# Scan, attention and gathering in one block, and a feed-forward's last turn by token halves

## What is computed

```python
# second block
y_sc  = sc_b * causal_dwconv(sc_c * sc_h, w_sconv)                  # 256 wide
o     = gated_delta_rule_chunked(l2norm(gq), l2norm(gk), gv, g, beta)   # 4 heads of 128: the scan
y_gdn = rmsnorm(o, w_gdn_norm) * silu(gz)                           # 512 wide: the gating
y_sb  = stick_breaking_attention(sq, sk, sv)                        # 4 heads of 64
x = x + concatenate([y_sc, y_gdn, y_sb]) @ w_mix_out                # 1024 x 1024
u = causal_dwconv(rmsnorm(x, w_norm_ffn) @ w_ffn_up, w_ffn_conv)    # 3 taps; first block: no convolution
gate, val = split(u)                                                # 2816 each
x = x + (silu(gate) * val) @ w_ffn_down
out = rmsnorm(x, w_norm_final)
# stick breaking: A[t,s] = sigmoid(z_ts) * prod_{s<j<t} (1 - sigmoid(z_tj)), z = q.k/sqrt(64), s < t
```

## Time and profile before

| | |
|---|---|
| median of 3 runs | 2931.18 us (2931.16 to 2939.09) |
| profiled execution | 2928.09 us, span of the core 2926.4 us |
| TensorE busy | 2715.1 us, 93% |
| VectorE, ACT, POOL busy | 1306.2 (45%), 658.8 (23%), 1150.9 us (39%) |
| mean granted TensorE clock | 0.974 of full speed |

### The profile page before, as it was taken

How to read it: one execution, slowest core, us unless ns; L and a number is a source line. 1 busy time by engine, 2 the same in 40 slices (tenths; PEclk the granted TensorE clock), 3 DMA queues, 4 the chain that set the end, 5 groups by cost and what they waited for, 6 DMA issues and landing times. The chain is left out here.

```text
span 2926.4 us, 35051 instructions
## 1 busy us (share of the span) xinstructions
PE 2715.1 (93%) x12987; PEld 2175.6 (74%) x12987; DVE 1306.2 (45%) x1819; ACT 658.8 (23%) x1173; POOL 1150.9 (39%) x901
## 2 busy tenths in 40 slices
PE   4999887999999999969999888879899999999996
PEld 2888446888888888857888677854588888888885
DVE  4022542323343333371351356667234555666556
ACT  2110661300010000051232233235222211111113
POOL 2443026234444444433454323200523554555551
PEclk9999998999999999989999899989999999999998
DMA  3110103111111111121111000000311111111111
GB/s 103 44 51 27 40 15 130 29 44 47 47 50 50 47 50 47 57 73 47 51 47 44 1 1 1 1 1 1 130 30 37 49 44 49 50 50 47 50 54 65
DMA packets 91204, 131.53 MB, mean 45 GB/s; under 512 B 9461, under 2 KB 57824, under 8 KB 91112
## 3 DMA queue, kind: packets, MB, share of 16 engines
q1 hardware_dynamic: 88808, 121.88, 13.9%
q10 hardware_dynamic: 2304, 8.39, 0.7%
HBM read 121.82 MB, written 8.42 MB: 45 GB/s over the span
## 5 line engine op out<-in xcount | busy, mean ns | idle before, releaser
L123 POOL TENSOR_TENSOR w_hi<-w_raw,zero 128x512 fp32r<-128x512 f32 x352 | 417.6, 1186 | 1198.4 <-PE bank L980 473.5
L125 POOL TENSOR_TENSOR w_lo<-w_raw,w_hi 128x512 fp32r<-128x512 f32 x352 | 511.8, 1454 | 27.6
L978 PE MATMUL bank<-xt_hi,w_hi 128*128 128x512 f32 x1312 | 510.6, 389 | 1.6 <-DVE x_sb L1156 0.8
L979 PE MATMUL bank<-xt_lo,w_hi 128*128 128x512 f32 x1312 | 510.4, 389 | 0.0
L980 PE MATMUL bank<-xt_hi,w_lo 128*128 128x512 f32 x1312 | 510.4, 389 | 0.0
L1254 DVE TENSOR_TENSOR x_sb<-bank,x_sb 128x512 f32<-128x512 f32 x320 | 221.3, 691 | 213.9 <-PE bank L1014 213.9
L978 PEld LDWEIGHTS bank<-xt_hi,w_hi 128*128 128x128 f32 x1312 | 246.3, 188 | 53.5 <-DVE x_sb L1156 1.3
L980 PEld LDWEIGHTS bank<-xt_hi,w_lo 128*128 128x128 f32 x1312 | 246.3, 188 | 51.2
L979 PEld LDWEIGHTS bank<-xt_lo,w_hi 128*128 128x128 f32 x1312 | 246.3, 188 | 51.0
L177 PE MATMUL bank<-xt_hi,w_hi 128*128 128x512 f32 x512 | 199.4, 389 | 0.0
L177 PE MATMUL bank<-xt_lo,w_hi 128*128 128x512 f32 x512 | 199.2, 389 | 0.0
(11 more groups left out here) (412 smaller groups left out, 4513.2 us busy)
## 6 DMA issues: line engine op xcount, KB each, us to landing
w_raw<-in_w_gate_up_dram SPq DMA_DIRECT2D x88, 256.0 KB, 3.1
w_raw<-in_w_ffn_up_dram SPq DMA_DIRECT2D x88, 256.0 KB, 3.1
w_raw<-in_w_mix_in_dram SPq DMA_DIRECT2D x48, 256.0 KB, 2.7
w_raw<-in_w_down_dram SPq DMA_DIRECT2D x44, 256.0 KB, 2.6
w_raw<-in_w_ffn_down_dram SPq DMA_DIRECT2D x44, 256.0 KB, 2.6
w_raw<-in_w_in_dram SPq DMA_DIRECT2D x40, 256.0 KB, 2.7
x_sb<-in_x_dram SPq DMA_DIRECT2D x8, 512.0 KB, 7.3
gate_rows<-gate_sums SPq DMA_DIRECT2D x8, 512.0 KB, 4.9
```

Of the source, the lines that this page charges most:

```text
L123: pool.tensor_tensor(m.w_hi[:, u, :], m.w_raw[:, u, :], zeros, ALU.add).then_inc(m.hi_done, 1)
L125: pool.tensor_tensor(m.w_lo[:, u, :], m.w_raw[:, u, :], m.w_hi[:, u, :].bitcast(F32), ALU.subtract).then_inc(m.split, 1)
L978: pe.matmul(m.psum[b][:, :], u_hi[:, col], m.xt_hi[:, k, tok], start=k == 0, stop=False)
L979: pe.matmul(m.psum[b][:, :], u_hi[:, col], m.xt_lo[:, k, tok], start=False, stop=False)
```

## The change

1. `scan_stage`, `stick_stage` and `gather_stage` become one block, `read_stage`. The attention's buffers get addresses of their own. The last chunk's update of the state is left out. In the scan ACT squares each head's output with an accumulated sum just behind its copy, for the 1/rms. POOL scales and gates `gz`, eight tiles each, makes the convolution's `xt_lo` and splits the next stage's first four slices, which SP loads. ACT rounds the convolution's rows. Finished attention outputs go from the bank into `xt_hi` (ACT) and `xt_lo` (VectorE) at once. The transposes of `gz` stand in the last two steps (first four groups) and behind them (last four), in the banks of the scores.
2. In both `mlp_stage`s the loop has a pass less. The last up product takes token half 0 through all eight slices, then half 1. Slices 4 to 7 go to `end_hi`, `end_lo`, so that all eight stay in SBUF; the last hidden rows go to `last_hi`, `last_lo`. ACT and VectorE make half 0 of the last hidden rows beside half 1 of the up product, and half 1 beside the down product before the last, VectorE with a step after each bank that it reads. POOL's split for the next stage waits until the last rescale.
3. In `proj2_stage` the chunk made of two column pieces is loaded with one DMA per slice.

The diff, cut (in `read_stage`, `L` is the number of steps):

```diff
+    end_hi, end_lo = m.at("end_hi" + tag, [P, 4, HALF], 152, F32R), m.at("end_lo" + tag, [P, 4, HALF], 160, F32R)
+    last_hi, last_lo = m.at("last_hi" + tag, [P, 2, S], 168, F32R), m.at("last_lo" + tag, [P, 2, S], 8, F32R)
+    spare = [m.at(f"scaled_out{i}" + tag, [P, 4, D], (16, 152)[i]) for i in range(2)]
...
-            with sp.Fori(0, FI - 1) as i:
+            with sp.Fori(0, FI - 2) as i:
                 up_slices(loop + 12 * i, i + 1)
                 down_slices(loop + GU + 12 * i, i)
+            up_slices(last, FI - 1)
+            down_slices(last + GU, FI - 2)
...
-            down_slices(loop + 12 * (FI - 1), FI - 1)
+            down_slices(last + 12, FI - 1)
...
-            split_slices(m, pool, loop, 12 * FI - 8)
+            split_slices(m, pool, loop, 12 * (FI - 2))
+            for k in range(GU):
+                u, n = k % RING, last + k
+                if k < RING:
+                    split_slice(m, pool, n, n // RING, u, False)
+                else:
+                    pool.wait_ge(m.loaded[u], 16 * (n // RING) + 16)
+                    pool.tensor_tensor(end_hi[:, u, :], m.w_raw[:, u, :], zeros, ALU.add).then_inc(m.hi_done, 1)
+                    pool.wait_ge(m.hi_done, n + 1)
+                    pool.tensor_tensor(end_lo[:, u, :], m.w_raw[:, u, :], end_hi[:, u, :].bitcast(F32),
+                                       ALU.subtract).then_inc(m.split, 1)
+            for u in range(DN):
+                n = last + GU + u
+                pool.wait_ge(m.used, last + u + 1)
+                split_slice(m, pool, n, n // RING, u, True)
+            split_slices(m, pool, last + 12, DN)
...
+                pool.wait_ge(scl, 2 * NT)
...
                 up(loop + 12 * i, wait_bank)
                 down(loop + GU + 12 * i, i)
-            pe.wait_ge(m.split, loop + 12 * (FI - 1) + 4)
+            for h in range(2):
+                for k in range(KD):
+                    pe.wait_ge(m.split, last + k + 1)
+                    for b in range(4 * h, 4 * h + 4):
+                        if k == 0:
+                            pe.wait_ge(ev_d if b % 2 else ev_a, 4 * (FI - 2) + b // 2 + 1)
+                            pe.wait_ge(dn_ev, 16 * (FI - 2) + b + 1)
+                        if k < RING:
+                            up_bank(last, k, m.w_hi[:, k, :], m.w_lo[:, k, :], b)
+                        else:
+                            up_bank(last, k, end_hi[:, k % RING, :], end_lo[:, k % RING, :], b)
+            down(last + GU, FI - 2)
+            pe.wait_ge(m.split, last + 12 + DN)
...
+            def finish_half(h):
+
+                i, tok = FI - 1, slice(h * HALF, (h + 1) * HALF)
+                if conv:
+                    act.wait_ge(ev_a, 4 * i + 2 * h + 2)
+                    act.wait_ge(ev_d, 4 * i + 2 * h + 2)
+                    for c in range(4):
+                        act.activation(mix[:, c, tok], raw[:, c, PAD + h * HALF:PAD + (h + 1) * HALF], ACT.Identity,
+                                       scale=weights_of(i, c, 2)).then_inc(tap, 1)
+                    for c in range(2):
+                        act.wait_ge(acted, 4 * i + 4 * h + c + 1)
+                        act.activation(mix[:, c, tok], mix[:, c, tok], ACT.Silu).then_inc(sig, 1)
+                for j in range(2):
+                    act.wait_ge(hid_a, 4 * i + 2 * h + j + 1)
+                    act.activation(last_hi[:, j, tok], mix[:, j, tok], ACT.Copy).then_inc(sig2, 1)
...
+                        if last_step is not None and NT * nh + t < STEPS:
+                            last_step(1, NT * nh + t)
...
+            TAPS = 8 if conv else 0
+            STEPS = TAPS + 4
+
+            def last_step(h, n):
...
+                i, tok = FI - 1, slice(h * HALF, (h + 1) * HALF)
+                pad = slice(PAD + h * HALF, PAD + (h + 1) * HALF)
+                j = n % 2
+                if n < TAPS:
+                    c, back = n // 2, 1 + j
+                    if back == 1:
+                        dve.wait_ge(tap, 4 * i + 4 * h + c + 1)
+                    else:
+                        dve.wait_ge(mid, 4 * i + 4 * h + c + 1)
+                    dve.scalar_tensor_tensor(
+                        mix[:, c, tok], raw[:, c, PAD - back + h * HALF:PAD - back + (h + 1) * HALF],
+                        weights_of(i, c, 2 - back), mix[:, c, tok], ALU.mult, ALU.add).then_inc(mid if back == 1 else acted, 1)
+                elif n < TAPS + 2:
+                    if conv:
+                        dve.wait_ge(acted, 4 * i + 4 * h + 4)
+                        dve.wait_ge(sig, 2 * i + 2 * h + 2)
+                    else:
+                        dve.wait_ge(ev_a, 4 * i + 2 * h + 2)
+                        dve.wait_ge(ev_d, 4 * i + 2 * h + 2)
+                    a_, u_ = (mix[:, j, tok], mix[:, 2 + j, tok]) if conv else (raw[:, j, pad], raw[:, 2 + j, pad])
+                    dve.tensor_tensor(mix[:, j, tok], a_, u_, ALU.mult).then_inc(hid_a, 1)
+                else:
+                    dve.wait_ge(hid_a, 4 * i + 2 * h + 2)
+                    dve.wait_ge(sig2, 4 * i + 2 * h + j + 1)
+                    dve.tensor_tensor(last_lo[:, j, tok], mix[:, j, tok], last_hi[:, j, tok].bitcast(F32),
+                                      ALU.subtract).then_inc(hid, 1)
...
+            with dve.Fori(0, FI - 2) as i:
                 read_up(loop + 12 * i, i + 1)
                 read_down(loop + GU + 12 * i, i)
                 finish(i + 1)
+            read_up(last, FI - 1, (0, 1))
+            for n in range(STEPS):
+                last_step(0, n)
+            read_up(last, FI - 1, (2, 3))
+            read_down(last + GU, FI - 2, last_step)
...
+                    apart = pieces[c][1][0] - col
+                    before = apart - 256
+                    load_slices(m, sp, base, 8 * c, 8, lambda j, u: (
+                        m.w_raw[:, u, :].rearrange("p (s n) -> p s n", s=2),
+                        w[bass.ds((j * RING + u) * P, P), col - before:col - before + 2 * apart]
+                        .rearrange("p (s n) -> p s n", s=2)[:, :, before:apart]))
...
-            split_slices(m, pool, base, 32, RING)
-            for k in range(KD):
-
-                pool.wait_ge(two[k % RING], 16 * (k // RING + 1))
-                if k % RING == RING - 1:
-                    split_slices(m, pool, base + 32 + k - RING + 1, RING)
-            split_slices(m, pool, base + 40, 16)
+            split_slices(m, pool, base, 8 * NC, RING)
...
+def read_stage(m, q_, k_, v_, t_at, gz, sc, sqk, sv, first):
...
+    zc, sp, acc, A = (m.at(n, [P, 4, HALF], 120 + 8 * i) for i, n in enumerate(("z_capped", "softplus", "later", "weights")))
...
+            pool.wait_ge(rs_done, 2)
+            for c in range(NT):
+                g4 = gz[:, c, :].rearrange("p (h n) -> p h n", h=HG)
+                pool.tensor_tensor(g4, g4, rs[:, c, :].unsqueeze(2).to_broadcast([P, HG, P]), ALU.mult).then_inc(scaled, 1)
+            for c in range(NT):
+                pool.wait_ge(scaled, c + 1)
+                pool.tensor_tensor(gz[:, c, :], gz[:, c, :], o[:, c, :, :].rearrange("p h n -> p (h n)"),
+                                   ALU.mult).then_inc(gated, 1)
+            pool.wait_ge(gated, NT)
+            for k in range(2):
+                pool.wait_ge(sc_hi, k + 1)
+                pool.tensor_tensor(m.xt_lo[:, k, :], sc[:, k, :], m.xt_hi[:, k, :].bitcast(F32), ALU.subtract)
+            split_first(m, pool, m.slices)
...
+                if c < NT - 1:
+                    for h in range(HG):
+                        pe.matmul(m.psum[h][:, 0:P], kd[:, h, c, :], vn[:, h, :], start=True, stop=True).then_inc(pe_s, 1)
...
+                if p == 2:
+                    pe.wait_ge(act_s, 4 * NT)
...
+            def turn_gates(i):
+
+                h, k = i // 4, i % 4
+                if i < 6:
+                    pe.wait_ge(weighed, 2 * (L - 3 + i // 2) + i % 2 + 1)
+                else:
+                    pe.wait_ge(g_lo, i - 5)
+                pe.wait_ge(gated, NT)
+                for j in range(4):
+                    mm = pe.transpose(m.psum[turn_bank(i)][:, j * P:(j + 1) * P], gz[:, 4 * h + j, k * P:(k + 1) * P],
+                                      m.ident[:, :])
+                mm.then_inc(g_turn, 1)
...
+            for p in range(L):
                 sums(p)
-                if p + 2 < len(steps):
+                if p + 2 < L:
                     scores(p + 2)
+                else:
+                    for i in range(2):
+                        turn_gates(2 * (p + 2 - L) + i)
                 if p:
                     values(p - 1)
-            values(len(steps) - 1)
+            values(L - 1)
+            for i in range(4, 8):
+                turn_gates(i)
...
+            def output_low(p):
+                g, b, q = steps[p]
+                if b == 0:
+                    tok = slice(g * HALF, (g + 1) * HALF)
+                    dve.wait_ge(y_hi, 2 * g + q + 1)
```

(53 more changed lines are left out.)

230 lines of the change are left out of this document (78 added, 152 removed).

## The result

| | before | after |
|---|---|---|
| median | 2932.19 us (4 runs, 2931.16 to 2939.09) | 2906.69 us (4 runs, 2899.54 to 2911.94) |
| ratio, 95% interval | | 0.9901, 0.9875 to 0.9928 |
| profiled execution (span) | 2928.09 (2926.4) | 2911.94 (2910.2) |
| mean granted clock | 0.974 | 0.971 |

The kernel is faster by 25.5 us; the forecast of 2887 was 20 us too low and its range (2876 to 2902) ended 4.7 us short.

A forecast was written before the change was run, and what follows sets the result against it. TensorE, busy 93% of the span, was taken as the bound, leaving only idle and half-clock time. Terms 27.9+13.5-3.5+3.2+3.0 = 44.1 us took the profiled 2928.1 to 2884.0, a median of 2887 us; range 2876 to 2902.

The forecast's parts named there:

- Part 1: Scan to attention: scores start 19.8 us sooner, and 0.5 us more from starting at full clock.
- Part 2: Work moved beside the attention: POOL's contention with VectorE costs 4 us (0 to 10), the output order 1 us.
- the middle's order: Mid-attention outputs go ACT high, then VectorE low, with the next softplus queued behind: 1 us lost (0 to 3).
- Part 3: Attention to second feed-forward: the wait of 17.7 us shrinks by 11.6 us, plus 1 us from the clock.
- Rival A: Contention: POOL beside the attention costs its full 10 us, with other losses, gain 31 us, 2900 us; chance 0.20.
- The clock's microsecond: Second feed-forward's start: after under 3 us of idling TensorE may start at full clock, half of 2.1 counted, 1 us.
- Part 4: Feed-forwards' last turn by token halves: 13.5 us gained in the second, 3.2 in the first, late slices cost 3.5.
- Part 5: First feed-forward's end: POOL's split waits for the last rescale, so ACT's squares set the end, 3.0 us gained.
- B: Better rival: no contention price, slices in time, both clocks kept in the second feed-forward; gain 55.4, 2876 us; chance 0.14.
- C: Slower rival: TensorE's instructions come late in the last turn's straight code; 2945 us at 0.10 us each; chance 0.03.
- D: No-gain rival: VectorE or ACT bounds all 24 attention steps, 1.6 us more each, 2925 us; chance 0.03.
- the one that was named as proving it wrong: In the attention: TensorE's waits for softplus growing by more than 10 us would show the forecast wrong.

The follow-up runs named there:

- pool_late: The changed kernel with POOL's whole work of the scan and attention block held back until the attention's sixteenth step; 2893.43 us (0.9873).
- all_late: The changed kernel with POOL's work held back and cut to 128 columns, output low after softplus, last slices in buffers of their own; 2878.38 us (0.9814).
- read_only: The changed kernel with both feed-forward blocks as before the change; 2917.66 us (0.9943).
- all_early: The changed kernel with POOL's work cut to 128 columns at its early place, output low after softplus, last slices in own buffers; 2889.51 us (0.9852).
- after_again: The changed kernel, unaltered, run again in a second set; 2905.02 us (0.9904).

## Why the prediction was wrong, step by step

**Part 1, right but for its clock.** 19.8 us forecast; 23.6 minus 3.5 is 20.1. ACT's squares stayed hidden: from the scan's first product to its last it is 28.9 us before and after. The half microsecond for a full clock at the first scores didn't come: with POOL's work held back, the first interval is 4.3 and 4.2 us (pool_late, all_late), and 4.1 before.

**Part 2, contention: the step that failed.** It took VectorE's 2.25 us against 1.27 as a factor, applied that to some 13 us of small operations and so had 10 as its upper end, of which it chose 4. Measured: 131.4 - 115.2 = 16.2 us, of which the middle's order is 2.0, so 14.2 for POOL's work (which itself took 32.2 us, not 35 to 60). The row that was used didn't bear that reading. POOL's rows of before that lie beside it, which the prediction left out:

```profile
1290.50 1.28 POOL L125 TENSOR_TENSOR w_lo<-w_raw,w_hi 128x512 fp32r<-128x512 f32 x1
...
1291.74 2.02 POOL L123 TENSOR_TENSOR w_hi<-w_raw,zero 128x512 fp32r<-128x512 f32 x1
```

VectorE started at 1290.62 and was held until POOL's instruction ended at 1291.78, 1.16 us; it then ran until 1292.87, while POOL's next, 1.04 us alone, was held in its turn. So the 2.25 is 1.27 plus nearly all of the rest of one POOL instruction (0.98 of 1.16), no factor. A held operation pays that rest however small it is, so what had to be counted was VectorE's instructions (20 of them beside POOL in the first steps, 0.73 us each), not their microseconds. The reason for taking the low end failed too: it went by TensorE's full wide steps, while POOL's 30 us fall into the narrow ones, where VectorE sets the pace. Rival A had named just this place; the 5.1 us that TensorE waited in the old attention were held against it, but they show no slack on VectorE.

The prediction weighed a page of the Trainium skill, the GPSIMD Engine Reference (Key points), that names which operations meet. Another page of the Trainium skill, SBUF — State Buffer (Who interferes with whom), says how: the pair of ports is locked for a whole instruction and the other engine blocks fully, it isn't a shared bandwidth. The trace agrees (1.28 and 1.30 us beside 1.31 and 1.26).

The middle's order was charged 1 us of 0 to 3 and cost 2.0. The transposes in the last two steps cost their 1.8.

**Part 3, right in the main.** 17.7 to 5.4 is 12.3 us. But the sum holds one 1.8 for transposes, and there are two: sixteen lengthen the attention, sixteen stand in the seam, where 6 us were named as the sign. If the one in the sum is the attention's, as in the 6.3 above, the seam was forecast at 13.4; either way the part gained 12.3 - 1.8 = 10.5, where 11.6 was written. The clock's microsecond didn't come: from the block's first product to its first one with `big_hi`, 13.6 us against 13.1. The granted clock 3 to 5 us into the block, beside the earlier trace rows:

```profile
2080.00:2082.00 2.00, 2.00 (x7) 1.52 (x6) 0.00 (x0) 0.00 (x0) 1.38 (x2) 0.50 1.02 406
```

After 3.5 us of idling TensorE ran at 0.50, the lower of its two levels (1.2 GHz), here. In two experiments with the same 3.5 us (read_only, all_early) the clock was granted at 1.00 from the first product on and the stretch took 11.0 us; in five others it took 12.6. So the term can come, worth 2.1 us, but the length of the idling alone doesn't tell whether it does; what does stays open.

**Part 4, right.** 4.2 us of wait for POOL's slice before both last down products, as written (its own subtraction, 2882.1 less 2878.0, gives 4.1). The slices late in the half pass cost 2.1 us in two waits. The forecast named three, of 0.9, 1.5 and 1.5 us, and put their sum at 3.5; it is 3.9. The second feed-forward gained 9.5 to 11.1 us, and 10.6 behind its first stretch (823.7 to 813.1); forecast 10.0. Leaving the clock behind this wait uncounted was right: over some 4 to 5 us it was granted at 0.63 before, behind 17.7 us of waiting, and at 0.62 after, behind 4.2.

**Part 5, right.** With Part 4's 3.2 the first feed-forward was to gain 6.2; it gained 6.5 in every kernel that has the edit. The squares follow one another at 1.6 us.

**The stages left alone.** The sum set them at nothing, against the one profiled execution of before. But the same code took 494.1 to 500.6 us in the first attention and 260.5, 263.2 to 263.9 or 270.3 to 270.4 in the delta stage. Stretches of the delta stage, before, after and after_again:

```profile
1639.00:1899.00 260.00, 218.46 (x1536) 192.96 (x1534) 164.23 (x273) 84.91 (x135) 90.88 (x58) 0.92 0.00 1
```

```profile
1637.10:1907.40 270.30, 230.64 (x1536) 202.89 (x1536) 164.62 (x273) 85.86 (x136) 91.81 (x63) 0.87 0.00 1
```

```profile
1635.50:1898.90 263.40, 223.36 (x1537) 196.86 (x1537) 164.52 (x273) 85.95 (x136) 91.95 (x65) 0.91 0.00 1
```

The same code, VectorE's time the same to 0.4 us; TensorE's busy time follows the granted clock. The profiled execution of before happened to have both stages at their shortest; measured from it every comparison looks worse. Of the 28 us by which the profiled execution of after missed its 2884, 13.5 are Parts 1 to 3 (27.9 forecast, 14.4 measured) and 16.2 these two stages, less 1.8 elsewhere (1.5 of it ahead of TensorE's first instruction). Of the 13.5, the attention is 11.7 (18.0 against 6.3), the clock behind the second seam 1.0 and the seams the rest. In the medians 13.5 of 19.6 us are explained in this way; the other 6 are less than what these two stages vary by (6.5 and 9.9 us), but that they are theirs is argued, not shown. What decides which length a run gets isn't settled: with the same code there, no edit here goes with one of them.

**The rivals.** A, contention, at 2900 had the mechanism at too low a price, from the same factor: 10 and 3, where 14.2 and 2.0 were measured. With those it would have given 2903. B, C and D didn't happen: the last turn's straight-line products follow one another at 0.227 us as elsewhere, and the full wide intervals are 5.7 us before and after. The range failed with the forecast: its upper end, 2902, took A in only to its middle. Of the signs listed, the one that was named as proving it wrong came near: TensorE's waits for the softplus grew by 8.9 us where the bound was set at 10. That sign was badly chosen, as time lost to a clock that falls doesn't show as waiting.

## What to carry to other kernels

Before work is moved to POOL beside a stage, find who sets the pace there; if it is VectorE, count its instructions that read two SBUF tiles or copy in SBUF, and charge each with the rest of one POOL instruction, not with a percentage. If the work must stand there, put it beside the steps in which VectorE's instructions are few and long, and cut POOL's instructions to about the length that may be lost: here that turned a loss of 14 us into none. And set a sum against medians of stages from several executions where the stages can differ by clock alone; one profile's luck was worth as much as a term of this sum.
